# Convolution of the sample tokens moved from TensorE to Pool and VectorE, prompt groups narrowed from 168 to 128 columns

## The reference, cut to what matters

```python
def conv_branch(u, hist, w_dw, b_dw, ln_g, ln_b):
    full = jnp.concatenate([hist, u], axis=1)          # hist: 30 rows, zero for the prompt
    c = lax.conv_general_dilated(full, w_dw[:, None, :], (1,), 'VALID',
                                 feature_group_count=CONV_CH, ...) + b_dw
    c = layernorm(c, ln_g, ln_b)
    c = c * jax.nn.sigmoid(c)
    return c, full[:, -(CONV_WIDTH - 1):]
```

## Time and profile before

| | |
|---|---|
| median of three runs | 1568.78 us |
| the profiled execution | 1569.07 us |
| its span | 1566.9 us |
| PE, PEld busy | 1497.9 us (96%), 1255.5 us (80%) |
| DVE, ACT, POOL busy | 678.9 us (43%), 603.9 us (39%), 439.1 us (28%) |

### The profile page before, as it was taken

How to read it: one execution, slowest core, us unless ns; L and a number is a source line. 1 busy time by engine, 2 the same in 40 slices (tenths; PEclk the granted TensorE clock), 3 DMA queues, 4 the chain that set the end, 5 groups by cost and what they waited for, 6 DMA issues and landing times.

```text
span 1566.9 us, 22129 instructions
## 1 busy us (share of the span) xinstructions
PE 1497.9 (96%) x8490; PEld 1255.5 (80%) x8490; DVE 678.9 (43%) x1322; ACT 603.9 (39%) x1081; POOL 439.1 (28%) x451
## 2 busy tenths in 40 slices
PE   7998999999899998899999999999999999999995
PEld 4466356654788764478799999999999999999995
DVE  2438467878935564435532222222222222222234
ACT  4217549886447765644331221212112021120211
POOL 3233014442613433423321121121122112112124
PEclk9999999999999999999999999999999999999998
DMA  7021141447481006340021111111111111111112
GB/s 241 1 59 58 49 90 76 164 120 97 173 260 63 2 9 257 139 155 1 1 62 47 41 43 52 40 40 54 40 40 42 52 40 42 52 40 40 55 41 101
DMA packets 95635, 116.65 MB, mean 74 GB/s; under 512 B 15142, under 2 KB 80758, under 8 KB 92996
## 3 DMA queue, kind: packets, MB, share of 16 engines
q1 hardware_dynamic: 92076, 94.72, 20.1%
q0 software_dynamic: 3488, 20.98, 3.6%
HBM read 95.05 MB, written 20.95 MB: 74 GB/s over the span
## 4 chain that ended last, share of the span: by engine, by line
PE 55%; POOL 1%; DVE 1%; DMA 0%; issue 0%; ACT 0%; DVEq 0%; POOLq 0%; ACTq 0%
PE ps L2375 18%; PE ps L2377 18%; PE ps L2376 18%; PE ps L2410 0%; POOL y L2270 0%; DVE y L2545 0%; DMA out_y_p<-y 0%; POOL wlo L2234 0%; PE ps L2462 0%; DVE y L2555 0%; POOL stat L2245 0%; ACT whi L2284 0%; ACT hhi L2342 0%; POOL stat L2241 0%; DVEq L2544 0%
## 5 line engine op out<-in xcount | busy, mean ns | idle before, releaser
L2234 POOL TENSOR_TENSOR wlo<-wraw,whi 128x1024 fp32r<-128x1024 f32 x62 | 149.0, 2403 | 566.4 <-ACT whi L2284 566.3
L2376 PE MATMUL ps<-xlo,whi 128*128 128x384 f32 (+1 forms) x768 | 250.3, 326 | 0.0
L2375 PE MATMUL ps<-hhi,whi 128*128 128x384 f32 (+1 forms) x720 | 235.1, 327 | 0.8 <-POOL wlo L2234 0.8
L2377 PE MATMUL ps<-hhi,wlo 128*128 128x384 f32 (+1 forms) x720 | 235.2, 327 | 0.0
L2376 PE MATMUL ps<-hlo,whi 128*128 128x384 f32 (+1 forms) x720 | 234.9, 326 | 0.0
L2284 ACT CAST whi<-wraw 128x1024 fp32r<-128x1024 f32 x62 | 65.2, 1052 | 293.8 <-PE ps L2377 293.8
L2522 DVE TENSOR_TENSOR rel<-rel 128x384 f32<-128x384 f32 (+1 forms) x96 | 51.5, 537 | 283.7 <-ACT rel L2350 283.7
L2350 ACT ACTIVATE rel<-ps 128x384 f32<-128x384 f32 (+1 forms) x96 | 45.3, 473 | 264.3 <-PE ps L2377 264.3
L2376 PEld LDWEIGHTS ps<-xlo,whi 128*128 128x128 f32 x768 | 144.1, 188 | 0.0
L2375 PEld LDWEIGHTS ps<-hhi,whi 128*128 128x128 f32 x720 | 135.2, 188 | 1.1 <-POOL wlo L2234 1.1
L2377 PEld LDWEIGHTS ps<-hhi,wlo 128*128 128x128 f32 x720 | 135.1, 188 | 0.0
(11 more groups left out here) (316 smaller groups left out, 2795.7 us busy)
## 6 DMA issues: line engine op xcount, KB each, us to landing
wraw<-in_w_up SPq DMA_DIRECT2D x32, 512.0 KB, 4.0
wraw<-in_w_down SPq DMA_DIRECT2D x32, 512.0 KB, 3.4
taps<-qT SPq DMA_DIRECT2D x9, 960.0 KB, 4.0
hT<-taps SPq DMA_DIRECT2D x7, 960.0 KB, 4.9
x<-in_x SPq DMA_DIRECT2D x13, 512.0 KB, 7.3
w<-in_w_u SPq DMA_DIRECT2D x2, 2048.0 KB, 8.0
wo_raw<-in_w_out SPq DMA_DIRECT2D x8, 512.0 KB, 4.2
out_y_p<-y SPq DMA_DIRECT2D x8, 512.0 KB, 2.6
```

Of the source, the lines that this page charges most:

```text
L2234: nc.gpsimd.tensor_tensor(wlo_of(j, last), raw[:], whi_of(j, last), ALU.subtract).then_inc(s_wlo, 1)
L2375: nc.tensor.matmul(o, wh, xh, start=first, stop=False)
L2376: nc.tensor.matmul(o, wh, xl, start=False, stop=False)
L2377: return nc.tensor.matmul(o, wl, xh, start=False, stop=last)
```

## The change

- The samples' 40 columns leave the groups: a group is 132 columns in and 128 out (XT, XO), `by_channel` and `by_time` shrink with it, four groups share a bank (CONV_BANK 4, so 8 events in place of 11), and ACT takes an event with one copy.
- `usm` is no longer a tile in phase layout that Pool clears and SP writes to DRAM; it is the plain history and new rows, channel by channel, in the unused end of `up`. ACT fills it with one copy for each half, Pool adds the new rows. Its former place as a buffer of the tie step goes to a tile `tie1`, and the tie step no longer waits for the write to DRAM.
- At attention's start the depthwise weights are loaded (`dwn`), and Pool multiplies, for each of four channel tiles and two halves of the samples, a 4 x 8 x 31 window of `usm` by the weights (`prods`, two buffers). DVE sums the 31 products with one reduction each, behind the mask step of heads 1 to 8, into the samples' columns of `conv`. The bias of a channel tile waits for its two sums.
- `conv` is read from DRAM into the prompt's 128 columns of each phase only.
- The load of output weights 1 waits for the eighth product.

```diff
-XP = (HIST + 2 + SEQ) // PH
-XS = (HIST + 2 + NT) // PH
-XT = XP + NB * XS
-XRUN = XT - XS + 1
-XO = T // PH
+XT = (HIST + 2 + SEQ) // PH
+XO = SEQ // PH
-CONV_BANK = 3
+CONV_BANK = 4
+UP_ROOM = 172
...
             for h in range(2):
                 cs2 = slice(2 * h, 2 * h + 2)
                 sp.wait_ge(s_um, len(uunits) // 2 * (h + 1))
-                sp.wait_ge(s_un, 2 * (h + 1))
-                sp.dma_start(by_channel[:, cs2, :, 0:XP], upr[:, cs2, :, :]).then_inc(s_iw, 16)
-                sp.dma_start(by_channel[:, cs2, :, XP:XT], usm[:, cs2, :, :]).then_inc(s_iw, 16)
-                sp.wait_ge(s_iw, 32 * (h + 1))
+                sp.dma_start(by_channel[:, cs2, :, :], upr[:, cs2, :, :]).then_inc(s_iw, 16)
+                sp.wait_ge(s_iw, 16 * (h + 1))
...
-            sp.dma_start(conv[:, 0:2, :].rearrange("p c (o x) -> p c o x", o=PH), by_time[:, 0:2, :, :]
-                         ).then_inc(s_co, 16)
+            sp.dma_start(conv[:, 0:2, :].rearrange("p c (o x) -> p c o x", o=PH)[:, :, :, 0:XO],
+                         by_time[:, 0:2, :, :]).then_inc(s_co, 16)
...
         @block.gpsimd
         def _(pool):
-            nc.gpsimd.memset(usm[:], 0.0).then_inc(s_zero, 1)
...
             def take_history(e):
                 act.wait_ge(s_tr, e + 1)
-                act.wait_ge(s_zero, 1)
-                dst = usm[:, :, :, e * hb * XS:(e + 1) * hb * XS].rearrange("p c s (b x) -> p c b x s", x=XS)
-                nc.scalar.copy(dst[:, :, :, 0, 2:PH], src[:, :, :, 0:PH - 2])
-                for c in range(CC):
-                    last = nc.scalar.copy(dst[:, c, :, 1:XS - 1, :],
-                                          src[:, c, :, PH - 2:HIST].rearrange("p b (x s) -> p b x s", s=PH))
-                last.then_inc(s_te, 1)
+                nc.scalar.copy(usm[:, :, e * hb:(e + 1) * hb, 0:HIST], src).then_inc(s_te, 1)
...
             def take_conv(k):
-                nc.scalar.copy(up[:, g0:g0 + ng, 0:SEQ // PH], src[:, :, 0:SEQ // PH])
-                late = src[:, :, SEQ // PH:].rearrange("p g (b x) -> p g b x", x=XS)[:, :, :, XS - 1]
-                nc.scalar.copy(up[:, g0:g0 + ng, SEQ // PH:XO], late).then_inc(s_ce, 1)
+                nc.scalar.copy(up[:, g0:g0 + ng, 0:XO],
+                               bank[2 + EVENTS.index(("c", k)) % 6].rearrange("p (g x) -> p g x", x=XO)[:, 0:ng, :]
+                               ).then_inc(s_ce, 1)
...
-                        last = nc.tensor.matmul(o, wdiag[g][:, j * P:(j + 1) * P], up[:, g, j:j + XRUN],
+                        last = nc.tensor.matmul(o, wdiag[g][:, j * P:(j + 1) * P], up[:, g, j:j + XO],
                                                 start=(j == 0), stop=(j == STEPS - 1))
...
             dve.wait_ge(s_u, len(uunits))
-            dve.wait_ge(s_iw, 16 * 4)
...
# phase_attend, SP
             for c in range(2, 4):
                 for r in range(PH):
                     sp.dma_start(by_time...)
+            sp.dma_start(dwn, a["dw"]).then_inc(s_c, 16)
             sp.dma_start(ones[:], a["ones"]).then_inc(s_c, 16)
             sp.wait_ge(s_ow, 16 * 4 * PH)
-            sp.dma_start(conv[:, 2:4, :].rearrange("p c (o x) -> p c o x", o=PH), m["by_time"][:, 2:4, :, :]
-                         ).then_inc(s_co, 16)
+            sp.dma_start(conv[:, 2:4, :].rearrange("p c (o x) -> p c o x", o=PH)[:, :, :, 0:XO],
+                         m["by_time"][:, 2:4, :, :]).then_inc(s_co, 16)
...
             load_out(0, s_wo[0])
+            sp.wait_ge(s_pr, N_PR + 2 * CC)
             load_out(1, s_wo[0])
# phase_attend, Pool, behind the four gathers
+            pool.wait_ge(s_c, 32)
+            for c in range(CC):
+                for h in range(2):
+                    if c >= 1:
+                        pool.wait_ge(s_ys, N_YS + 2 * c + h - 1)
+                    x = usm[:, c, h * HB:(h + 1) * HB, 0:NT]
+                    window = bass.AP(x.tensor, x.offset, list(x.ap) + [[1, CW]])
+                    weights = dwn[:, c, :].unsqueeze(1).unsqueeze(1).broadcast_to([P, HB, NT, CW])
+                    nc.gpsimd.tensor_tensor(prods[h], window, weights, ALU.mult).then_inc(s_pr, 1)
+            pool.wait_ge(s_pr, N_PR + 2 * CC)
# phase_attend, DVE
+            def sum_sample(k):
+                c, h = k // 2, k % 2
+                dve.wait_ge(s_pr, N_PR + k + 1)
+                dve.wait_ge(m["s_iw"], 16 * 2)
+                y = conv[:, c, :].rearrange("p (o x) -> p x o", o=PH)[:, XO + h * HB:XO + (h + 1) * HB, :]
+                nc.vector.tensor_reduce(y, prods[h], AX_X, ALU.add).then_inc(s_ys, 1)
...
                         accum_out=mx[:, j % 4:j % 4 + 1]).then_inc(s_m, 1)
+                    if 1 <= j <= 2 * CC:
+                        sum_sample(j - 1)
                     if 2 * NH <= j < 2 * NH + CC:
                         c = j - 2 * NH
+                        dve.wait_ge(s_ys, N_YS + 2 * (c + 1))
                         dve.wait_ge(s_co, 16 * (c // 2 + 1))
```

More of the change, by code:

```diff
@@ L155, in build @@
             m["mask"] = sb_in(qkv, "mask", [P, MK_COLS], BF16)
-            m["up"] = sb_in(qkv, "up", [P, NCG, XT])
+            up = sb_in(qkv, "up", [P, NCG * UP_ROOM])
+            m["up"] = up[:, 0:NCG * XT].rearrange("p (g x) -> p g x", x=XT)
+            m["usm"] = up[:, NCG * XT:NCG * XT + CC * NB * (HIST + NT)].rearrange("p (c b x) -> p c b x", c=CC, b=NB)
             m["kT"] = sb_in(qkv, "kT", [P, T])
@@ L235, in phase_project @@
     s_wu = m["s_wu"] = sem("p_wu")
-    m["p_x"], m["p_w"] = s_x, s_w
+    m["p_x"], m["p_w"], m["p_first"], m["p_const"] = s_x, s_w, s_first, s_const
     s_sq = sem("p_sq")
@@ L697, in phase_select @@
     conv = moT[:, CC:KC, :]
-    upr = conv.rearrange("p c t -> p (c t)")[:, 0:CC * PH * XP].rearrange("p (c s x) -> p c s x", c=CC, s=PH)
-    usm = sb_in(st, "usm", [P, CC, PH, NB * XS])
+    upr = conv.rearrange("p c t -> p (c t)")[:, 0:CC * PH * XT].rearrange("p (c s x) -> p c s x", c=CC, s=PH)
+    usm = m["usm"]
+    tie1 = sb_in(st, "tie1", [P, KEYS // 2])
     wq = wslot[0]
@@ L745, in phase_select @@
     tie = [used[:, KEYS:KEYS + KEYS // 2].bitcast(BF16),
-           usm[:].rearrange("p c s x -> p (c s x)")[:, 0:KEYS // 2].bitcast(BF16)]
+           tie1[:].bitcast(BF16)]
     sets = [(P, scores[:, SC_OFF[i]:SC_OFF[i] + P * (i + 1)], mask[:, MK_OFF[i]:MK_OFF[i] + P * (i + 1)])
@@ L768, in phase_select @@
     s_ql = m["s_ql"] = sem("s_ql")
-    s_iw = sem("s_iw")
+    s_iw = m["s_iw"] = sem("s_iw")
     s_ow = m["s_ow"] = sem("s_ow")
@@ L844, in _ @@
             sp.dma_start(hist[:], a["state_conv"].rearrange("(s r) c -> r s c", s=2)).then_inc(s_h, 16)
-            sp.wait_ge(s_zero, 3)
+            sp.wait_ge(s_zero, 2)
             dw4 = a["dw"].rearrange("(q h) c j -> h q c j", q=PH)
@@ L937, in _ @@
                     pool.wait_ge(s_um, q + 1)
-                    nc.gpsimd.tensor_copy(usm[:, c, :, :].rearrange("p s (b x) -> p b s x", x=XS)[:, :, :, XS - 1],
+                    nc.gpsimd.tensor_copy(usm[:, c, :, HIST:HIST + NT],
                                           unew[:, c, :].rearrange("p (b t) -> p b t", t=NT)).then_inc(s_un, 1)
@@ L1018, in take_conv @@
                 act.wait_ge(s_cg, g0 + ng)
-                src = bank[2 + EVENTS.index(("c", k)) % 6][:, 0:CONV_BANK * XRUN].rearrange("p (g x) -> p g x", x=XRUN)[:, 0:ng, :]
-                nc.scalar.copy(up[:, g0:g0 + ng, 0:SEQ // PH], src[:, :, 0:SEQ // PH])
-                late = src[:, :, SEQ // PH:].rearrange("p g (b x) -> p g b x", x=XS)[:, :, :, XS - 1]
-                nc.scalar.copy(up[:, g0:g0 + ng, SEQ // PH:XO], late).then_inc(s_ce, 1)
+                nc.scalar.copy(up[:, g0:g0 + ng, 0:XO],
+                               bank[2 + EVENTS.index(("c", k)) % 6].rearrange("p (g x) -> p g x", x=XO)[:, 0:ng, :]
+                               ).then_inc(s_ce, 1)
             for it in range(BITS):
@@ L1147, in convolve @@
                         pe.wait_ge(s_fetch[n % 3], N_FETCH[n % 3] + 16 * (n // 3 + 1))
-                    o = bank[2 + e % 6][:, (g % CONV_BANK) * XRUN:(g % CONV_BANK + 1) * XRUN]
+                    o = bank[2 + e % 6][:, (g % CONV_BANK) * XO:(g % CONV_BANK + 1) * XO]
                     for j in range(STEPS):
-                        last = nc.tensor.matmul(o, wdiag[g][:, j * P:(j + 1) * P], up[:, g, j:j + XRUN],
+                        last = nc.tensor.matmul(o, wdiag[g][:, j * P:(j + 1) * P], up[:, g, j:j + XO],
                                                 start=(j == 0), stop=(j == STEPS - 1))
@@ L1326, in phase_attend @@
     csum = probS[:, 0:T]
+    HB = NB // 2
+    usm = m["usm"]
+    prods = [probS[:, h * HB * NT * CW:(h + 1) * HB * NT * CW].rearrange("p (b t j) -> p b t j", b=HB, t=NT)
+             for h in range(2)]
+    dwn = spread[:].rearrange("p q t -> p (q t)")[:, 0:CC * CW].rearrange("p (c j) -> p c j", c=CC)
     LNB = NBLK // 2
@@ L1372, in phase_attend @@
     s_add = sem("a_add")
+    s_pr, N_PR = m["p_first"], 16 * 3
+    s_ys, N_YS = m["p_const"], 16 * 6
```

(2 more changed lines are left out.)

## The result

The changed kernel takes 1578.38 us (median of four, 1577.22 to 1579.08), the kernel before 1568.27 us beside it (median of four too); the ratio is 1.0059 with a 95% interval of 1.0042 to 1.0076. It is slower by 10.1 us. The forecast was 1583.5, its range 1574 to 1590.

What follows compares the result with a forecast made beforehand. PE, busy 96% of the span, was taken as the bound. 1569.07 - 9.7 (groups) - 1.0 (copies) + 23.9 (delayed scores) + 1.5 (clock) = 1583.8 us, as a median 1583.5; range 1574 to 1590.

Steps and rivals of the forecast that it cites:

- Record pace: PE's convolution at the selection's end: a 128-column record every 0.109 us in place of 0.143, PE done 11.4 us earlier.
- The selection as a whole: Narrower groups gain 9.7 us and ACT's history copies 1.0: 10.7 us from both parts.
- Up to 422.9 us nothing is gained: PE's early convolution events: turns wait for Pool's rotations; four 128-column groups take 4.4 us, three of 168 took 4.44.
- ACT's copies: Search rounds: two history copies of some 1.0 us replace ten taking 2.0, gaining 1.0 us of path.
- The fetches: SP's tap fetches keep up with faster groups: a refill has 6.5 us, lands in 4.9, leaving 1.6.
- The landing of the loads: Attention's start: `dwn` and `ones`, behind SP's 16 writes, are there 24.5 us into the block; bounds 17 and 28.
- The small pieces: First read of `conv`, ahead of the writes: 512-byte pieces add 2.4 us to its landing; bounds 0 and 4.8.
- Product, sum, restart: Attention's first heads: product 2.3 us, sum 1.1, landing to head 4's scores 4.9, half-clock restart 1.5.
- Slow products: Rival: Pool's products take 5 us, so heads 3 to 8 come every 5 us in place of 3; 1598, chance 0.05.
- Pieces that cost nothing: Rival: the small pieces of the `conv` read cost nothing; chance 0.13.
- Fetches that don't keep up: Rival: tap fetches lag behind the faster groups, the gain falls from 9.7 to 4 us; 1589, chance 0.09.
- Loads that overtake the writes: Rival: small loads don't queue behind the writes at attention's start; 1558.4, chance 0.08 for landing below 7 us, 0.05 in between.

Runs made afterwards that it cites:

- the wait alone: Kernel before, with one added VectorE wait behind head 1's mask step for the load of the ones, no products or sums: 1584.95 us, ratio 1.0092.
- the run with late sums: Changed kernel with the eight sums behind the mask steps of heads 8 to 15 in place of 1 to 8: 1558.48 us, ratio 0.9940.

## Why the prediction was right, and which terms were off

The mechanism was the one forecast, step by step: the narrower groups free 9 to 10 us, the first sum blocks VectorE's list until SP's late loads are in, PE stands idle, resumes at a granted clock of 0.50, and makes nothing up. The forecast was 5.1 us too high in the median, and the experiments show by which terms.

- **Record pace.** Taken 0.109 us, measured 0.112; PE's last stretch became 10.7 us shorter where 11.4 stood. SP's list, not PE, ends the block, as forecast: the writes start at 429.35, the read of `conv` is issued 10.9 us later (11.1 taken).
- **The selection as a whole** gained 12.7 us against this profile, where 10.7 stood, and 3.5 of it are not the change's: the unchanged selection took 243.5, 243.5 and 240.0 us in the three profiles that have it (the third is that of the wait alone), the changed one 230.4 to 230.8 in all six. The two slower ones have the clock dip at 379 us, 1.6 us; and in the quicker one Pool's rotations fall otherwise between DVE's tie steps, so that PE waits 4.3 us for Pool in place of 6.0. Like for like the gain is 9.2 to 9.6 us, a little under the 10.7. "Up to 422.9 us nothing is gained" was wrong in the form: the turn that waits for Pool came sooner.
- **ACT's copies** became 1.0 us in place of 2.0, as forecast, but the 31 rounds ended only 0.4 us sooner (163.4 us after the first clearing of `cand`, before 163.8): 0.4 where 1.0 stood.
- **The fetches** kept up but for one place that I had not looked at: the fourth group of the first event is the first that needs a fetch, and PE waits 0.39 us for it.
- **The landing of the loads** is the step that was mis-sized: 24.5 us into the block in the forecast, 18.75 measured. I had added 2.4 us for the small pieces of the read ahead and 1.5 for its shorter head start to the 20.6 of the profile. The pieces cost the read about 1 us, and in the run that has only them the ones landed at 20.2: no delay of the loads is seen, though a scatter of 2.6 us could hide 1. Nor does 20.6 hold as a base: the same code gave 18.0 in another execution. The part of the landing that the runs show is that of the 16 writes against the gathers (11.2 us without these). Whether the head start plays any part was not tried by itself.
- **The small pieces.** The pieces of 512 and 544 bytes cost a read about 1 us of 5.2, where 2.4 stood. The row from which the 2.4 came, a write, had another write beside it: in the changed kernel, alone, the same write of `by_channel`, still in pieces of 528 bytes, lands in 5.0 to 5.1 us where it took 7.5 and 9.6. So that row did not show what pieces cost.
- **Product, sum, restart.** 2.13 us (14.90/7) for a product where 2.3 stood, 1.18 for a sum where 1.1 stood, 4.6 us from the landing to head 4's scores where 4.9 stood; the clock's loss 1.8 us at head 6 where 1.5 stood. Over the heads 18.4 us were lost in all, 1.3 less than at head 6; that is the clock dip at head 48 in the profile before, and no time made up.
- **The rivals.** Slow products: refuted by 2.13 us and by the run with late sums. Pieces that cost nothing (chance 0.13): not quite (about 1 us for the read), but no run shows that cost in the loads' landing or in the total. Fetches that don't keep up: one wait of 0.39 us. Loads that overtake the writes: they were issued behind them and landed with them, the weights 18.0 us into the block, the last write at 18.4, the ones at 18.75.

In the sum the landing gives -5.8 us against the forecast, the selection -2.0, the restart and the later heads -1.3; the first phase and the samples' clock dips, which are scatter, +4.0, and the time outside the span -0.4; together -5.5, where the profiled execution came out 5.4 below the sum. How near the forecast came is in part luck: the +4.0 are scatter and hide part of the landing's error. And the two dips in the profile before make most of the -2.0 and the -1.3: like for like the selection gained 1.1 to 1.5 us less than forecast, and the landing is the one large error.

## What to carry to other kernels

A wait costs what stands behind it in its engine's list, not what the waiting instruction does: 1.2 us of sum cost 18 us, and four heads further down the list, with its load ahead of the writes, it cost nothing that can be seen. Before work is put into the cover of an early stage, look up when its first input can be there: its place in the issuing list, and what else the DMA engines carry then (the loads landed 18.8 us into the block beside the gathers, 11.2 without them). And where events alternate with a wait for another engine, fill them until the wait is gone (four groups in place of three: 4.4 us).

## What the runs showed of the hardware

- A Pool product of 64 columns, 0.31 us at its shortest, took up to 4.45 us in the tie step while a DVE scan of 4.51 us ran (changed kernel and wait alone; 3.87 us before). How the two lists fell together moved PE's waits for Pool by 1.7 us from one execution of the same code to another.
- 64 KB loads queued behind 1 MB of writes in pieces of 512 or 544 bytes landed 18.0 to 20.6 us after the block's start with 4 MB of gathers in flight, and 11.2 us without.
- After 9 to 17 us of idle PE ran some 3 to 6 us at a granted clock of 0.50, at a loss of 0.9 to 1.8 us (five runs). Behind the search rounds, at head 48 and in the samples' part the granted clock dips to 0.50 in some executions and not in others, for 3 to 10 us in all at each and at a loss of 1 to 4 us, a good part of this kernel's scatter.
